# Attention scores of a one-core decoder step: queries and keys split into a high part and a remainder, and the normalized v kept in the buffer of v

## The reference

```python
scores = jnp.einsum('bnqkgd,bnskd->bnkgqs', qb, kk,
                    preferred_element_type=jnp.float32) * (HEAD_DIM ** -0.5)
...
vn = layernorm(vg, gmlp_ln_g[l], gmlp_ln_b[l])
gm = gmlp_prompt(u, vn, gmlp_w_s[l], gmlp_b_s[l])
```

## Time and profile before

| | us |
|---|---|
| median of 3 runs (lowest, highest) | 716.06 (715.21, 717.71) |
| the profiled execution's own time | 715.4 |
| its span, first to last instruction | 713.7 |
| PE busy in the span | 692.3 |
| DVE busy | 555.3 |
| ACT busy | 451.4 |
| a steady tile of stage 1 | 28.13 |

### The profile page before, as it was taken

How to read it: one execution, slowest core, us unless ns; L and a number is a source line. 1 busy time by engine, 2 the same in 40 slices (tenths; PEclk the granted TensorE clock), 3 DMA queues, 4 the chain that set the end, 5 groups by cost and what they waited for, 6 DMA issues and landing times.

```text
span 713.7 us, 11899 instructions
## 1 busy us (share of the span) xinstructions
PE 692.3 (97%) x3816; PEld 540.9 (76%) x3816; DVE 555.3 (78%) x890; ACT 451.4 (63%) x714; POOL 152.3 (21%) x157
## 2 busy tenths in 40 slices
PE   7999999999999999999988999999999999999995
PEld 4777777887778778777777888888888888888842
DVE  4775866866858875363887999999999999999857
ACT  7645354453465643122245888898889888898745
POOL 1010010110110131000014233333333333341114
PEclk9999999999999999999999999999999999999998
DMA  9993830330311626635339999999999999998758
GB/s 350 267 308 96 196 89 0 88 88 0 88 59 68 237 96 235 261 128 187 112 137 353 415 415 412 411 392 388 403 392 381 380 393 393 366 404 339 268 197 357
DMA packets 80922, 181.10 MB, mean 254 GB/s; under 512 B 41720, under 2 KB 45984, under 8 KB 72696
## 3 DMA queue, kind: packets, MB, share of 16 engines
q1 hardware_dynamic: 71384, 163.12, 63.0%
q0 software_dynamic: 9216, 16.93, 6.3%
q10 hardware_dynamic: 288, 0.62, 0.3%
HBM read 162.89 MB, written 34.39 MB: 276 GB/s over the span
## 4 chain that ended last, share of the span: by engine, by line
PE 85%; DVE 4%; DMA 4%; ACT 2%; issue 2%; SPq 1%; POOL 1%; DVEq 0%; ACTq 0%; POOLq 0%
PE psZ L1391 24%; PE psZ L901 20%; PE psS L1418 12%; PE psZ L1092 10%; PE psT L831 6%; PE psOG L831 2%; PE psOG L974 2%; PE psS L942 2%; DMA wo_in<-w_out 1%; PE psOG L1223 1%; PE psOG L983 1%; DMA yy<-y_d 1%; PE psOG L873 1%; DVE x1a L2692 1%; PE psT L1181 1%
## 5 line engine op out<-in xcount | busy, mean ns | idle before, releaser
L2388 DVE TENSOR_TENSOR wg_lo<-wg,wg_hi 128x1024 fp32r<-128x1024 f32 x128 | 150.7, 1218 | 2.0 <-ACT wg_hi L1531 2.0
L1531 ACT ACTIVATE wg_hi<-wg 128x1024 fp32r<-128x1024 f32 x128 | 128.8, 1062 | 3.6 <-DVE small L2550 1.6
L1391 PE MATMUL psZ<-wg_hi,xg_hi 128*128 128x512 f32 x252 | 101.4, 402 | 0.0
L1391 PE MATMUL psZ<-wg_hi,xg_lo 128*128 128x512 f32 x252 | 99.0, 393 | 0.0
L1391 PE MATMUL psZ<-wg_lo,xg_hi 128*128 128x512 f32 x252 | 99.0, 393 | 0.0
L901 PE MATMUL psZ<-wi_hi,xT_hi 128*128 128x512 f32 (+1 forms) x240 | 90.0, 375 | 1.0 <-DVE wi_lo L1963 1.0
L2774 POOL DMA_INDIRECT y_d<-y_t,idx_dst x32 | 48.9, 1528 | 188.5 <-ACT y_t L1531 188.5
L2577 DVE TENSOR_TENSOR wd_lo<-wd,wd_hi 128x2048 fp32r<-128x2048 f32 x31 | 71.1, 2292 | 21.0 <-ACT wd_hi L1531 21.0
L901 PE MATMUL psZ<-wi_lo,xT_hi 128*128 128x512 f32 (+1 forms) x240 | 87.2, 364 | 0.0
L901 PE MATMUL psZ<-wi_hi,xT_lo 128*128 128x512 f32 (+1 forms) x240 | 87.2, 363 | 0.0
L2770 POOL DMA_INDIRECT xg<-h_d,idx_src x32 | 58.5, 1830 | 22.2 <-issue 13.7
(11 more groups left out here) (354 smaller groups left out, 1346.3 us busy)
## 6 DMA issues: line engine op xcount, KB each, us to landing
wg<-w_gate SPq DMA_DIRECT2D x32, 1024.0 KB, 9.9
wg<-w_up SPq DMA_DIRECT2D x32, 1024.0 KB, 17.4
wd<-w_down SPq DMA_DIRECT2D x32, 1024.0 KB, 13.1
y_d<-wo_stage SPq DMA_DIRECT2D x1, 4608.0 KB
wi_raw<-w_in SPq DMA_DIRECT2D x4, 1024.0 KB, 14.1
x_t<-x_rows SPq DMA_DIRECT2D x8, 512.0 KB, 4.0
mix_d<-mix_t SPq DMA_DIRECT2D x8, 512.0 KB, 3.0
m_t<-mix_d SPq DMA_DIRECT2D x8, 512.0 KB, 3.7
```

The source lines that it names most:

```text
L1391: last = nc.tensor.matmul(psZ[z][:], a[:, c, :], w, start=(n == 0), stop=(n == 3 * DC - 1))
L1531: return nc.scalar.activation(out, in_, ACT.Copy)
L2388: tt(wg_lo[k][:, :, c, :], wg[k][:, :, c, :], wg_hi[p][:].bitcast(F32), ALU.subtract).then_inc(s_wgl, 1)
```

## The change

Queries and keys of the prompt tiles are kept as a high part and a remainder, both fp32r. ACT's `q_out` writes the high part qT_hi; the remainder is made on DVE, in two halves, qT_lo[0] for the chunks of round 0 and qT_lo[1] for those of round 1. kT_s holds both parts of k: [:, 0] high, [:, 1] remainder, 256 columns each. DVE's `k_out` grows from one copy to a copy, a subtraction, and, after a wait for qT_hi, two subtractions that each raise s_kT; in tile 0 it also copies both parts to the left half. A round is q high x k high, q remainder x k high, q high x k remainder for each chunk and kv head: 12 products of 256 columns, in tile 0 too. Round 0 waits for the first q remainder, round 1 and `gm` for the second (psG holds q until then). `k_shift` moves both parts. The sample tile keeps f32 copies in the same memory.

The normalized v is written over vg_t, and vn_t is gone; the Gelu of the next tile waits for `gm` (s_gm) in place of s_vn. The memory freed takes kT_s and qT_lo[1]; qT_lo[0] lies in a gap.

```diff
--- before.py
+++ after.py
@@ -163,19 +163,21 @@
         wi_first = Region(nc, base, r2.at - 8 * D, r2.at).take("wi_first", [P, 2, 768], F32)
         x_t = r2.take("x_t", [P, D], F32)
         q_ro = r2.take("q_ro", [P, ATT], F32)
-        qT = r2.take("qT", [P, QPK, P], F32)
+        qT = Region(nc, base, r2.at, r2.at + 2 * D).take("qT", [P, QPK, P], F32)
+        qT_hi = r2.take("qT_hi", [P, QPK, P], F32R)
         a1 = r3.at
         mix_t = r3.take("mix_t", [P, D], F32)
         xT_hi = r3.take("xT_hi", [P, DC, P], F32R)
         xT = Region(nc, base, r3.at, r3.at + 4 * D).take("xT", [P, DC, P], F32)
         xT_lo = r3.take("xT_lo", [P, DC, P], F32R)
         k_ro = r3.take("k_ro", [P, P], F32)
-        kT = r3.take("kT", [P, 2 * P], F32)
+        kT = Region(nc, base, r3.at, r3.at + D).take("kT", [P, 2 * P], F32)
+        kT_s = r3.take("kT_s", [P, 2, 2 * P], F32R)
         v_t = r3.take("v_t", [P, 2, P], F32)
         v_new = r3.take("v_new", [P, P], F32)
         u_t = r3.take("u_t", [P, GW], F32)
         vg_t = r3.take("vg_t", [P, GW], F32)
-        vn_t = r3.take("vn_t", [P, GW], F32)
+        qT_lo = [Region(nc, base, 147456, 147456 + D).take("qT_lo0", [P, 2, P], F32R), r3.take("qT_lo1", [P, 2, P], F32R)]
         s_at = r3.at
         s_t = [r3.take(f"s_t{g}", [P, QPK, 2 * P], F32) for g in range(2)]
         s_end = r3.at
@@ -741,7 +743,7 @@
                     sp.wait_ge(s_v, T)
                     sp.dma_start(v_sample, v_new[0:N_SAMPLE, :]).then_inc(s_kvout, 16)
                     sp.wait_ge(s_vn, T)
-                    sp.dma_start(g_sample, vn_t[0:N_SAMPLE, :]).then_inc(s_kvout, 16)
+                    sp.dma_start(g_sample, vg_t[0:N_SAMPLE, :]).then_inc(s_kvout, 16)
                     load_expert(0)
                     sp.wait_ge(s_u, T)
                     load_wq(2)
@@ -929,19 +931,20 @@
             def scores(t, g):
                 if g == 0:
                     pe.wait_ge(s_qT, t + 1)
-                    pe.wait_ge(s_kT, t + 1)
+                    pe.wait_ge(s_kT, 2 * t + 1)
                     if isinstance(t, int) and t == 0:
                         pe.wait_ge(s_vg, 1)
                     else:
                         pe.wait_ge(s_sm, 2 * t)
                 else:
                     pe.wait_ge(s_sm, 2 * t + 1)
+                    pe.wait_ge(s_kT, 2 * t + 2)
                 for c in range(2):
-                    for kv in range(NKV):
-                        rows_ = slice(kv * HD, (kv + 1) * HD)
-                        last = nc.tensor.matmul(psS[:, (2 * kv + c) * 256 + keys(t):(2 * kv + c + 1) * 256],
-                                                qT[rows_, 2 * g + c, :], kT[rows_, keys(t):],
-                                                start=True, stop=True, skip_group_check=True)
+                    for n, (a, b) in enumerate(((qT_hi[:, 2 * g + c, :], 0), (qT_lo[g][:, c, :], 0), (qT_hi[:, 2 * g + c, :], 1))):
+                        for kv in range(NKV):
+                            rows_ = slice(kv * HD, (kv + 1) * HD)
+                            last = nc.tensor.matmul(psS[:, (2 * kv + c) * 256:(2 * kv + c + 1) * 256], a[rows_], kT_s[rows_, b, :],
+                                                    start=(n == 0), stop=(n == 2), skip_group_check=True)
                 last.then_inc(s_sc, 1)
 
             def t_p(t, g):
@@ -978,9 +981,10 @@
             def gm(t):
                 pe.wait_ge(s_vn, t + 1)
                 pe.wait_ge(s_qT, t + 1)
+                pe.wait_ge(s_kT, 2 * t + 2)
                 for g in range(NG):
                     d = slice((g % 2) * HD, (g % 2 + 1) * HD)
-                    last = nc.tensor.matmul(psG[d, (g // 2) * P:(g // 2 + 1) * P], vn_t[:, g * HD:(g + 1) * HD],
+                    last = nc.tensor.matmul(psG[d, (g // 2) * P:(g // 2 + 1) * P], vg_t[:, g * HD:(g + 1) * HD],
                                             wsT[:, g, :], start=True, stop=True, skip_group_check=True)
                 last.then_inc(s_gm, 1)
 
@@ -1032,7 +1036,7 @@
             def sample_scores(b):
                 if b == 0:
                     pe.wait_ge(s_qT, T)
-                    pe.wait_ge(s_kT, T)
+                    pe.wait_ge(s_kT, 2 * T_P + 1)
                     pe.wait_ge(s_sm, 2 * T_P)
                 for g in range(NKV):
                     r = slice(g * HD, (g + 1) * HD)
@@ -1611,7 +1615,7 @@
                     act.wait_ge(s_z, 4 * t + 4)
                     z, n = (psS[:, 512:1024] if isinstance(t, int) and t == 0 else psZ[1][:]), P
                 if not (isinstance(t, int) and t == 0):
-                    act.wait_ge(s_vn, t)
+                    act.wait_ge(s_gm, t)
                 nc.scalar.activation(vg_t[0:n], z, ACT.Gelu, scale=st[0:n, 2:3]).then_inc(s_vg, 1)
 
             def o_out(t):
@@ -1624,7 +1628,10 @@
                 act.wait_ge(s_qkTp, 2 * t + 1)
                 if not (isinstance(t, int) and t == 0):
                     act.wait_ge(s_sc, 2 * t)
-                copy(qT[:].rearrange("p c t -> p (c t)"), psS[:, 512:1024] if isinstance(t, int) and t == T_P else psG[:]).then_inc(s_qT, 1)
+                if isinstance(t, int) and t == T_P:
+                    copy(qT[:].rearrange("p c t -> p (c t)"), psS[:, 512:1024]).then_inc(s_qT, 1)
+                else:
+                    copy(qT_hi[:].rearrange("p c t -> p (c t)"), psG[:]).then_inc(s_qT, 1)
 
             def split_out(n):
 
@@ -2095,18 +2102,29 @@
                 dve.wait_ge(s_var, t + 1)
                 if not (isinstance(t, int) and t == 0):
                     dve.wait_ge(s_gm, t)
-                step(stt(out=vn_t[:], in0=vg_t[:], scalar=st[:, 3:4], in1=lng[:], op0=ALU.subtract, op1=ALU.mult))
+                step(stt(out=vg_t[:], in0=vg_t[:], scalar=st[:, 3:4], in1=lng[:], op0=ALU.subtract, op1=ALU.mult))
                 dve.wait_ge(s_lnr, t + 1)
-                stt(out=vn_t[:], in0=vn_t[:], scalar=st[:, 6:7], in1=lnb[:], op0=ALU.mult, op1=ALU.add).then_inc(s_vn, 1)
+                stt(out=vg_t[:], in0=vg_t[:], scalar=st[:, 6:7], in1=lnb[:], op0=ALU.mult, op1=ALU.add).then_inc(s_vn, 1)
 
             def k_shift(t):
                 dve.wait_ge(s_sc, 2 * t)
-                dve.wait_ge(s_kT, t)
-                step(cp(kT[:, 0:P], kT[:, P:2 * P]))
+                dve.wait_ge(s_kT, 2 * t)
+                step(cp(kT_s[:, :, 0:P], kT_s[:, :, P:2 * P].bitcast(F32)))
 
             def k_out(t):
                 dve.wait_ge(s_qkTp, 2 * t + 2)
-                cp(kT[:, P:2 * P], psS[:, 0:P]).then_inc(s_kT, 1)
+                if isinstance(t, int) and t == T_P:
+                    cp(kT[:, P:2 * P], psS[:, 0:P]).then_inc(s_kT, 1)
+                else:
+                    step(cp(kT_s[:, 0, P:2 * P], psS[:, 0:P]))
+                    step(tt(kT_s[:, 1, P:2 * P], psS[:, 0:P], kT_s[:, 0, P:2 * P].bitcast(F32), ALU.subtract))
+                    if isinstance(t, int) and t == 0:
+                        step(cp(kT_s[:, :, 0:P], kT_s[:, :, P:2 * P].bitcast(F32)))
+                    dve.wait_ge(s_qT, t + 1)
+                    for g in range(2):
+                        q = slice(2 * g * P, 2 * (g + 1) * P)
+                        tt(qT_lo[g][:].rearrange("p c t -> p (c t)"), psG[:, q],
+                           qT_hi[:].rearrange("p c t -> p (c t)")[:, q].bitcast(F32), ALU.subtract).then_inc(s_kT, 1)
 
             def split_out(n):
 
@@ -2184,7 +2202,7 @@
             def sample_products():
 
                 dve.wait_ge(s_qT, T)
-                dve.wait_ge(s_kT, T)
+                dve.wait_ge(s_kT, 2 * T_P + 1)
                 step(nc.vector.memset(prod[:], 0.0))
                 for g in range(NKV):
                     r = slice(g * HD, (g + 1) * HD)
@@ -2201,7 +2219,7 @@
 
                 dve.wait_ge(s_vn, T)
                 dve.wait_ge(s_u, T)
-                v3 = vn_t[0:N_SAMPLE, :].rearrange("p (g d) -> p g d", g=NG)
+                v3 = vg_t[0:N_SAMPLE, :].rearrange("p (g d) -> p g d", g=NG)
                 m3 = vg_t[0:N_SAMPLE, :].rearrange("p (g d) -> p g d", g=NG)
                 step(tt(m3, v3, w00[0:N_SAMPLE, :].unsqueeze(2).to_broadcast([N_SAMPLE, NG, HD]), ALU.mult))
                 step(tt(m3, m3, b00[0:N_SAMPLE, :].unsqueeze(2).to_broadcast([N_SAMPLE, NG, HD]), ALU.add))
```

## The result

| | before | changed |
|---|---|---|
| median (lowest, highest) | 716.06 (715.21, 717.71) | 720.84 (717.50, 722.95) |
| ratio to before, 95% interval | | 1.0053 (1.0035, 1.0071) |
| the profiled execution, its span | 715.4, 713.7 | 720.84, 719.1 |

The forecast was 717.8, the range 715.7 to 719.8. On a second chip the same kernel took 719.69 against 716.87, a ratio of 1.0036 (1.0015, 1.0058). By these ratios the change costs 3.8 and 2.6 us (the medians lie 4.8 and 2.8 apart), where 1.7 was forecast. The second chip's median, 719.69, lies just inside the range, so that the first one's lies outside is in part scatter.

What follows compares the result with a forecast made beforehand. TensorE (PE, 97% busy) was taken as the bound. Tile 0's 1.37, tile 1's 0.18 and the steady tiles' 0.2 gave 1.75, say +1.7 us, on the 716.06 median: 717.8, range 715.7 to 719.8.

Steps and rivals of the forecast that it cites:

- A round's price: Score rounds: 12 fp32r products running as 6 pairs take 0.89 us against 1.06 before, a gain of 0.17 per round.
- Tile 0's sum: Tile 0's first scores: +1.12 us from added DVE work before them, +0.25 from the longer round, together +1.37.
- Tile 1: Tile 1: round 0 starts 0.52 us later, both rounds give back 0.17 each, +0.18 in all; DVE not binding.
- Steady tiles: Tiles 2 to 6: round 0 +0.31 us, rounds -0.17 each, but DVE's pT binds: +0.04 per tile, +0.2 for five.
- Rival B: Tiles: DVE becomes the bound, softmax and pT 0.15 us later per tile, +1.2 in all, 719.0 us; chance 24%.
- Tile 7: Output projection: PE's 0.6 us wait for mT_lo absorbs +0.25 and -0.34, so 0; without that cover -0.1.
- Other edits: Wider k shift (+0.0 to 0.2 us on DVE, followed by idle time), normalized v in place, Gelu's wait: nothing added.
- A sign that was off: Tile 0 in the changed trace: PE's wait before scores would be near 2.1 us, for qT_lo.

Runs made afterwards that it cites:

- run 1: The changed kernel once more, unaltered, on a second chip: 719.69 us, ratio 1.0036 to the kernel before.
- 3: Changed kernel with GpSimd's wo remainder waiting for VectorE's last one: ratio 1.0041 to the kernel before.
- 4: Kernel before with three small DVE instructions ahead of tile 0's kT copy, no fp32r products: 718.03 us, ratio 1.0020.
- run 5: Changed kernel with tile 0 multiplying only the right 128 key columns and DVE's left copy gone: ratio 1.0030 to the kernel before.
- 2: Changed kernel with six 128x128 identity products ahead of tile 0's scores: 718.48 us, ratio 1.0025 to the kernel before.
- 6: Kernel of run 5 with products reordered, the wait for q's remainder ahead of the last four; half the high x high products lost: 715.51 us, ratio 0.9987.
- 7: Kernel of 6 with four 128x128 products in tile 0's wait for k: ratio 0.9987 to the kernel before.
- kernel 8: Kernel of 6 with one start per PSUM bank, so the whole computation is done: 715.10 us, ratio 0.9974 to the kernel before.
- Run 9: Kernel before with two small DVE instructions ahead of its last wo remainder, so that GpSimd's starts first: ratio 1.0088, +6.5 us.
- run 12: Kernel before with only normalized v put in the place of v: ratio 1.0007.

## Why the prediction was wrong

- **A round's price: right.** 0.90 us measured, 0.89 worked out from f32 pairs and full-array fp32r spacing. The halves pair, in loads and products.
- **Tile 0's sum: right on its own terms, and the step failed there.** "Together +1.37" was +1.38. But the step stopped at the end of the round. It lengthened PE's one wait and asked only what waits behind, not what TensorE's clock does behind an idle stretch. The clock fell to 1.2 GHz for 3.4 us: +1.54 in the profiled execution. Profiles 1, 3, 4 and 5 show it too, 2, 6, 7 and 8 its absence behind shorter waits. This term, put at nothing, is the largest that the forecast lacked. How much of it the average execution pays stays open.
- **Tile 1: right** (+0.23 for +0.18).
- **Steady tiles: mis-sized.** +0.08 to +0.13 each for +0.04. The wait of round 0 was as forecast (+0.34 for +0.31), but round 1 gave back 0.08 and not 0.17, since DVE's mix_t binds ahead of the transposes of u, a step ahead of pT; I had seen a wait for mix_t only in tile 0. Five tiles: +0.42 to +0.65 for +0.2. Rival B had DVE as the bound, at 0.75 for these five.
- **Tile 7: wrong in the profiled execution.** "Change only how long PE waits: 0" took the order of DVE's and POOL's remainders as given. In the usual order the term was 3.78 - 3.61 = +0.17 (run 1). When POOL starts 0.2 us ahead, it holds DVE, and that cost 4.50 - 3.78 = 0.7 us against run 1. Run 9 shows the mechanism. That the one profile in ten with this order is the changed kernel's is chance as far as the runs show, and how often the order turns in executions without a profile stays open.
- **Other edits at nothing: right for the normalized v** (run 12: a steady tile of 28.13, though its interval of -0.6 to +1.7 us is wide). The wider k shift was not tried alone.
- **A slip in rival B.** 5 x 0.15 and 0.15 on each of tiles 0 and 1 are 1.05, not 1.2.
- **A sign that was off.** PE's wait in tile 0 was to be near 2.1 us. It was 1.61 in this profile, because PE came to it 0.46 us later (its transposes of q start at 38.06, before at 37.60), and 1.97 and 2.06 in runs 1 and 3. The chain on DVE was as worked out.

Sum as it should have been: 1.38 + 0.23 + 0.42 to 0.65 = 2.0 to 2.3, tile 7 in the usual order 0.2, the clock 0 to 1.5, the turned order 0 to 0.7, so +2.2 to +4.7; measured +2.6 and +3.8 by the ratios. What I took for an unavoidable price, the 0.34 us wait for the remainder of q, was a matter of order: kernel 8 hides it and is 0.26% faster than the kernel before.

## What to carry to other kernels

When a change lengthens a wait of TensorE, look at the granted clock behind the nearest waits of similar length, and put a stretch at 1.2 GHz into the sum as a term with two values; in the profiles here it about doubled the cost of the wait. When an operand is split in parts, issue first the products whose parts come first, and wait for the last part in the middle of the round. And where two engines' instructions start within a few tenths of a microsecond and exclude each other, the order is a term of the sum with two values.

## What the runs showed of the hardware

- In tile 0 TensorE's granted clock fell for 3.4 us in the five profiles with a wait of 1.45, 1.61, 1.97, 2.06 or 2.21 us, and in none of the nine with a wait of 0.37 to 1.18. The fall began between 0.2 us before the end of the wait and 1.6 us after it. Behind 3.66 us in run 9, ahead of the output projection, it fell too.
- The length of a wait alone does not decide it. Ahead of the first expert's transposes of xg nine waits of 1.49 to 2.06 us were followed by no fall, and one of 1.88 us (run 8) was; in four other profiles (changed, runs 2, 3 and 9) the clock fell there at another point, before or among the products that fill the wait for the gather. What decides it there was not tried.
- DVE and POOL instructions between SBUF operands exclude each other whole: DVE's remainder takes 3.25 us instead of 1.22 (changed kernel), a copy of four columns 2.19 instead of 0.17 (run 9).
- Halving the columns of an fp32r round on half arrays, from 256 to 128, saved only 0.08 of 0.90 us (run 5).
- Running the two regions of a bank alternately instead of one after the other went with a round of 0.96 instead of 0.90 us; the order of the three products changed with it.
